# Sparse attention in a fused two-block kernel: the compression's value rows under the first scores, and the value products of a step in one group over eight buffers

## What is computed

```python
def compress(raw, j):                      # j = 0: keys, j = 1: values
    blk = raw[:, tok] + cmp_pos[j][None, None, :, None, :]
    blk = blk.transpose(0, 1, 3, 2, 4).reshape(B, n_cmp, N_KV_HEADS, CMP_BLOCK * HEAD_DIM)
    hid = jax.nn.gelu(blk @ cmp_w1[j] + cmp_b1[j])
    return hid @ cmp_w2[j] + cmp_b2[j]
...
s_cmp = jnp.einsum('btghd,bcgd->bghtc', q, k_cmp)
p_cmp = masked_softmax(s_cmp, cmp_end[None, :] <= pos[:, None])
o_cmp = jnp.einsum('bghtc,bcgd->btghd', p_cmp.astype(v_cmp.dtype), v_cmp)
...
o = gb[..., 0:1] * ocb + gb[..., 1:2] * o_sel + gb[..., 2:3] * o_win
```

## Time and profile before

| | before |
|---|---|
| median of 3 runs | 1528.6 us (1528.43 to 1529.43) |
| the profiled execution's own time | 1528.77 us |
| its span in the profile | 1527.1 us |
| TensorE busy | 1500.8 us, 98% |
| VectorE busy | 1067.8 us, 70% |
| ScalarE busy | 696.5 us, 46% |
| GpSimd busy | 271.9 us, 18% |
| granted TensorE clock | 0.999 |

### The profile page before, as it was taken

One profiled execution on the slowest core, in us unless ns is written; L12 is line 12 of the kernel. 1 busy time (PEld: TensorE's weight loads), 2 busy tenths in 40 slices (PEclk: granted clock), 3 DMA queues, 4 the chain that ended last, 5 costly groups with the idle time before them and its releaser, 6 DMA issues.

```text
span 1527.1 us, 20994 instructions
## 1 busy us (share of the span) xinstructions
PE 1500.8 (98%) x8228; PEld 1249.2 (82%) x8228; DVE 1067.8 (70%) x1617; ACT 696.5 (46%) x1206; POOL 271.9 (18%) x205
## 2 busy tenths in 40 slices
PE   6999999999999999989999999999999999999999
PEld 5788888888888897977878888888888898877777
DVE  6798689889988773259885685665635653688665
ACT  4453552322314454347775552332314443777761
POOL 0110013223232000059872011111100011010000
PEclk9999999999999999999999999999999999999999
DMA  9774257478585213330000254344432242111211
GB/s 340 269 263 164 83 212 261 168 250 300 187 285 183 91 53 131 118 116 2 2 2 29 83 193 164 111 153 160 144 108 86 91 162 83 56 55 63 86 74 56
DMA packets 114247, 207.54 MB, mean 136 GB/s; under 512 B 6361, under 2 KB 21990, under 8 KB 114150
## 3 DMA queue, kind: packets, MB, share of 16 engines
q1 hardware_dynamic: 113822, 206.09, 39.3%
q10 hardware_dynamic: 328, 0.12, 0.0%
HBM read 202.00 MB, written 4.19 MB: 135 GB/s over the span
## 4 chain that ended last, share of the span: by engine, by line
PE 95%; DVE 3%; ACT 1%; issue 1%; DMA 1%; SPq 0%; ACTq 0%; DVEq 0%
PE PS L2340 56%; PE PS L2293 20%; PE PS L2694 3%; PE PS L2721 2%; PE PS L2684 2%; PE PS L2501 1%; PE PS L2787 1%; PE PS L2624 1%; PE PS L2364 1%; PE PS L2772 1%; PE PS L2853 1%; PE PS L2875 1%; PE PS L2574 1%; DVE MROW L1448 1%; PE PS L2686 1%
## 5 line engine op out<-in xcount | busy, mean ns | idle before, releaser
L764 ACT ACTIVATE WH<-RAW 128x2048 fp32r<-128x2048 f32 (+1 forms) x102 | 191.2, 1885 | 338.8 <-DMA RAW<-in_ff_w_in_dram 221.2
L1327 DVE TENSOR_TENSOR WL<-RAW,WH 128x2048 fp32r<-128x2048 f32 (+1 forms) x98 | 249.1, 2565 | 73.2 <-ACT WH L764 72.9
L544 POOL PARTITION_ALL_REDUCE MROW<-MACC x25 | 118.5, 4739 | 591.0 <-DVE MACC L1362 504.4
L2340 PE MATMUL PS<-WH,HIDh 128*128 128x512 f32 (+1 forms) x576 | 217.7, 378 | 0.0
L2340 PE MATMUL PS<-WH,HIDl 128*128 128x512 f32 (+1 forms) x576 | 217.5, 378 | 0.0
L2340 PE MATMUL PS<-WL,HIDh 128*128 128x512 f32 (+1 forms) x576 | 217.5, 378 | 0.0
L2340 PE MATMUL PS<-HTh,WH 128*128 128x512 f32 (+1 forms) x520 | 202.6, 390 | 0.0
L2340 PE MATMUL PS<-HTl,WH 128*128 128x512 f32 (+1 forms) x520 | 202.6, 390 | 0.0
L2340 PE MATMUL PS<-HTh,WL 128*128 128x512 f32 (+1 forms) x520 | 202.5, 389 | 0.0
L2340 PEld LDWEIGHTS PS<-WH,HIDh 128*128 128x128 f32 x576 | 108.4, 188 | 20.5 <-issue 0.2
L2340 PEld LDWEIGHTS PS<-WL,HIDh 128*128 128x128 f32 x576 | 108.4, 188 | 20.2
(11 more groups left out here) (380 smaller groups left out, 3065.6 us busy)
## 6 DMA issues: line engine op xcount, KB each, us to landing
MRAW<-in_ada_w_dram SPq DMA_DIRECT2D x40, 1024.0 KB, 7.3
RAW<-in_ff_w_in_dram SPq DMA_DIRECT2D x32, 1024.0 KB, 5.3
RAW<-in_ff_w_out_dram SPq DMA_DIRECT2D x32, 1024.0 KB, 5.1
RAW<-in_w_in_dram SPq DMA_DIRECT2D x16, 1024.0 KB, 5.2
MRAW<-in_w_ada_dram SPq DMA_DIRECT2D x12, 1024.0 KB, 8.7
PIECE<-in_ada_w_dram SPq DMA_DIRECT2D x16, 512.0 KB, 9.8
MRAW<-in_kv_ada_w_dram SPq DMA_DIRECT2D x8, 1024.0 KB, 6.1
RAW<-in_kv_w_dram SPq DMA_DIRECT2D x6, 1024.0 KB, 5.6
```

Of the source, the lines that this page charges most:

```text
L544: pool.partition_all_reduce(MROW[:], acc[:], P, RADD).then_inc(m_red, 1)
L764: act.activation(rounded(u)[:, 0:width(u)], RAW[:, u % 4, 0:width(u)], ACT.Copy).then_inc(w_hi, 1)
L1327: dve.tensor_tensor(WL[:, u % 4, 0:width(u)], RAW[:, u % 4, 0:width(u)], rounded(u)[:, 0:width(u)].bitcast(F32), ALU.subtract).then_inc(w_ ...
L2340: mm = pe.matmul(po, a, b_, start=(k == 0 and i == 0), stop=(k == KT - 1 and i == len(ops) - 1), skip_group_check=len(ops) > 3)
```

## The change

It has three parts.

1. **The value rows move.** Half of `hidden_rows(1, 0)` goes behind the `W2K` products, and `hidden_rows(1, 1)` is cut into five pieces of 3, 3, 3, 3 and 4 products that go ahead of `scores(3)` to `scores(7)`. The gelu of the values is no longer taken from ScalarE's table: VectorE adds the biases and makes x + 0.044715 x^3 at t = 9 (`value_rows`), ScalarE takes exp of it at t = 10, VectorE finishes at t = 11 (`value_gelu`). The `W2V` products go from t = 3 to t = 14, VectorE's eviction of them from t = 5 to t = 15, GpSimd's copy of `VC` behind its weights of step 0, and the first product with `VC` to t = 18. The exp table is loaded right behind the second gelu of the keys.
2. **One group a step.** All products of L2721 of a step come at unit 6, in the order tile 1 branch 0, tile 1 branch 1, tile 0 branch 0, tile 0 branch 1. The turned weights have eight buffers in turn, two of them in the space of the queries of the first two pairs. A step raises the semaphore `a_pv` twice where it did three times.
3. **GpSimd** runs one small addition, whose result nobody reads, behind the reduction that ends at 486.5 us in the profile before. The buffers `PB` change places.

```diff
-    PB = [at(f"PB{i}", [P, 512], F32, o_rb + 2048 * i if i < 4 else o_mraw + 2048 * (i - 4)) for i in range(12)]
+    PB = [at(f"PB{i}", [P, 512], F32, o_mraw + 2048 * i if i < 8 else o_rb + 2048 * (i - 8)) for i in range(12)]
...
+    PT += [at(f"PT{6 + i}", [P, 512], F32, o_y + 2048 * i) for i in range(2)]
...
+        pool.tensor_tensor(SM[:, 47:48], EPST[:], EPST[:], ALU.add)
         pool.wait_ge(full, 4 * group_of["compress"])
...
+            if S == 0:
+                pool.wait_ge(kc_r, 3)
+                pool.tensor_copy(VC[32:64, :, HD:2 * HD], VC[0:32, :, 0:HD]).then_inc(vc_copies, 1)
+                pool.wait_ge(vc_copies, 1)
...
     def turned_of(u):
-        return PT[row(u) % 6] if u % PER else PTC[u // PER % 2]
+        return PT[row(u) % 8] if u % PER else PTC[u // PER % 2]
...
+        act.activation(SM[:, 44:45], EPST[:], ACT.Exp)
+        act.wait_ge(kc_f, 1)
...
+        def gelu_exp():
+
+            act.wait_ge(hc_b, 8)
+            act.activation(GE[:], GE[:], ACT.Exp, scale=-GELU_RATE * GELU_CUBE).then_inc(hc_b, 1)
...
+            if t == 10:
+                gelu_exp()
...
+        def value_rows():
+
+            dve.wait_ge(hc_f, 4)
+            dve.wait_ge(kc_f, 1)
+            b, v = SM[:, 42:44], HC[:].rearrange("p m (g c) -> p m g c", c=CMP)
+            ps = PS[:, 6:8, 1:129].rearrange("p m (g c) -> p m g c", c=32)[:, :, :, 0:CMP]
+            dve.tensor_tensor(b, PS[:, 6:8, 0], C1[:, C_B1 + 2:C_B1 + 4], ALU.add).then_inc(hc_b, 1)
+            dve.wait_ge(hc_b, 5)
+            dve.tensor_tensor(b, PS[:, 6:8, 128], b, ALU.add).then_inc(hc_b, 1)
+            dve.wait_ge(hc_b, 6)
+            for mo in range(2):
+                last = dve.tensor_scalar(v[:, mo], ps[:, mo], SM[:, 42 + mo:43 + mo], None, ALU.add)
+            last.then_inc(hc_r, 1)
+            dve.wait_ge(hc_r, 3)
+            dve.tensor_tensor(GE[:], HC[:], HC[:], ALU.mult).then_inc(hc_b, 1)
+            dve.wait_ge(hc_b, 7)
+            dve.scalar_tensor_tensor(out=GE[:], in0=GE[:], scalar=1.0 / GELU_CUBE, in1=HC[:],
+                                     op0=ALU.add, op1=ALU.mult).then_inc(hc_b, 1)
+
+        def value_gelu():
+
+            dve.wait_ge(hc_b, 9)
+            dve.tensor_scalar(GE[:], GE[:], 1.0, None, ALU.add).then_inc(hc_b, 1)
+            dve.wait_ge(hc_b, 10)
+            dve.reciprocal(GE[:], GE[:]).then_inc(hc_b, 1)
+            dve.wait_ge(hc_b, 11)
+            dve.tensor_tensor(HC[:], HC[:], GE[:], ALU.mult).then_inc(hc_r, 1)
...
-        hidden_rows(1, 0)
+        hidden_rows(1, 0, last=8)
...
-        hidden_rows(1, 1)
+        hidden_rows(1, 0, first=8)
...
-                pairs = ((1, 0, (u - 2, u)),) if i == 3 else ((1, 1, (u - 2, u)), (0, 0, (u - 4, u - 1)),
-                                                              (0, 1, (u - 4, u - 1)))
-                for blk, br, of in pairs:
+                for blk, br, of in ((1, 0, (u - 5, u - 3)), (1, 1, (u - 2, u)), (0, 0, (u - 4, u - 1)),
+                                    (0, 1, (u - 4, u - 1))):
...
+            if 3 <= t < 8:
+                hidden_rows(1, 1, 3 * (t - 3), 16 if t == 7 else 3 * (t - 2))
             if t < UNITS:
                 scores(t)
-            if t == 3:
+            if t == 14:
                 compressed_values()
-            if t == TURN_LAG:
+            if t == VALUES_LAG + 2:
                 pe.wait_ge(vc_copies, 1)
-            if 0 <= t - VALUES_LAG < UNITS and (t - VALUES_LAG) % PER in (0, 3, 6):
+                values(0)
+            elif t > VALUES_LAG and t - VALUES_LAG < UNITS and (t - VALUES_LAG) % PER in (0, 6):
                 values(t - VALUES_LAG)
```

More of the change, by code:

```diff
@@ L737, in summed @@
     def summed(u):
-        return 3 * (u // PER) + (1, 2, 3, 2, 3, 3, 3)[u % PER]
+        return 2 * (u // PER) + (2 if u % PER else 1)
     def before_in_pt(u):
-        return u - PER if u % PER else u - 2 * PER
+        if u % PER == 0:
+            return u - 2 * PER
+        r = row(u) - 8
+        return PER * (r // 6) + r % 6 + 1 if r >= 0 else -1
     SB_BANK, SB_COL, SB_AT = (0, 1, 0, 2), (0, 0, P, 0), (0, 512, P, 768)
@@ L1832, in dve_program, with hidden_bias @@
         chunk(kv_br(1), split=False)
-        def hidden_bias(j, mo):
-            ps, i = hidden(j, mo), 2 * j + mo
-            dve.wait_ge(hc_f, i + 1)
-            b = SM[:, 40 + i:41 + i]
-            dve.tensor_tensor(b, ps[:, 0:1], C1[:, C_B1 + i:C_B1 + i + 1], ALU.add).then_inc(hc_b, 1)
-            dve.wait_ge(hc_b, 2 * i + 1)
-            dve.tensor_tensor(b, ps[:, 128:129], b, ALU.add).then_inc(hc_b, 1)
-        hidden_bias(0, 0)
-        hidden_bias(0, 1)
-        hidden_bias(1, 0)
+        def hidden_bias(mo):
+            ps = hidden(0, mo)
+            dve.wait_ge(hc_f, mo + 1)
+            b = SM[:, 40 + mo:41 + mo]
+            dve.tensor_tensor(b, ps[:, 0:1], C1[:, C_B1 + mo:C_B1 + mo + 1], ALU.add).then_inc(hc_b, 1)
+            dve.wait_ge(hc_b, 2 * mo + 1)
+            dve.tensor_tensor(b, ps[:, 128:129], b, ALU.add).then_inc(hc_b, 1)
+        def value_rows():
[7 more added lines that the diff above has]
+            dve.wait_ge(hc_b, 6)
+            for mo in range(2):
+                last = dve.tensor_scalar(v[:, mo], ps[:, mo], SM[:, 42 + mo:43 + mo], None, ALU.add)
[12 more added lines that the diff above has]
+            dve.tensor_tensor(HC[:], HC[:], GE[:], ALU.mult).then_inc(hc_r, 1)
+        hidden_bias(0)
+        hidden_bias(1)
         dve.wait_ge(kc_full32, 1)
@@ L1850, in dve_program @@
         dve.tensor_tensor(KCl[:], KCF[:], KCh[:].bitcast(F32), ALU.subtract).then_inc(kc_r, 1)
-        hidden_bias(1, 1)
         def compressed_values():
@@ L1944, in dve_program @@
                 negmax(t)
-            if t == 5:
+            if t == 11:
+                value_gelu()
+            elif t == 15:
                 compressed_values()
@@ L2617, in pe_program, with hidden_rows @@
         chunk("A", HIDh, HIDl, mixed=True)
-        def hidden_rows(j, mo):
+        def hidden_rows(j, mo, first=0, last=16):
             pe.wait_ge((cw0_in, cw1_in[mo])[j], 16)
-            for m in range(16):
+            for m in range(first, last):
                 half = m // 8
@@ L2626, in hidden_rows @@
                                skip_group_check=True)
-            mm.then_inc(hc_f, 1)
+            if last == 16:
+                mm.then_inc(hc_f, 1)
         evicted(35)
```

39 lines of the change are left out of this document (18 added, 21 removed).

## The result

| | before | changed |
|---|---|---|
| median | 1528.84 us (1528.43 to 1529.43, 4 runs) | 1544.06 us (1543.17 to 1544.55, 4 runs) |
| the profiled execution's own time | 1528.77 us | 1544.13 us |
| its span | 1527.1 us | 1542.3 us |
| TensorE, VectorE, ScalarE, GpSimd busy | 1500.8, 1067.8, 696.5, 271.9 us | 1504.5, 1063.5, 696.2, 274.7 us |
| granted TensorE clock | 0.999 | 0.995 |

The ratio is 1.0098, 95% interval 1.0086 to 1.0111: slower by 15.2 us. The forecast was 1529.2 with an upper end of 1533.0, so it was wrong, and the cause has to be a large one.

The account below looks back on a forecast made before the run. TensorE's order, holes included, was taken to bound the kernel (95% of the chain of waits), with VectorE setting the pace at the loop's start. The terms -1.7 + 4.8 - 3.5 + 0.8 = +0.4 gave 1529.2 us, range 1525.3 to 1533.0.

Parts of the forecast that it names:

- part 2, one group a step: Attention steps: one group less costs TensorE 0.25 us less a step, over 14 steps 3.5 us earlier.
- Eight buffers are enough for no new wait: Attention steps: the copy of unit 3 needs only the group of the step before, written two iterations ahead; no cost.
- Rival 2: TensorE behind the long group: VectorE starves, steps stretch 0.3 us in each of 14, +4.2, 1533.4 us; chance 0.12.
- my own criterion: Attention steps: a step stretches once VectorE's 8.0 us of work and its idle exceed the new 8.8 us.
- Part 1 up to the first scores: Compression to first scores: 16 records instead of 32 lie before the scores, so they start 1.7 us earlier, at 665.64.
- Part 1, the start of the loop: Loop start to the group of t = 22: VectorE, full there, gets new work; 4.8 us later.
- The new work: VectorE at t = 9 and 11: additions, products and a reciprocal of 1.6 us for the value gelu, sum 4.2 us.
- The company on the port: Loop start: GpSimd's weights of step 0 beside four new VectorE operations cost 0.2 us each, 0.7 in all.
- rival 3: Loop start: each of four VectorE operations waits for a whole GpSimd operation, +2.5 and perhaps 1 more, 1532.7 us; chance 0.08.
- The tail: Last two attention steps: later group products cost 1.5 us, turns no longer waiting give back 0.7; 0.8 us later.
- Rival 1: Loop start: the value rows hide in VectorE's holes and TensorE limits t = 8 to 22; -3.5, 1525.3 us; chance 0.18.
- rival 4: GpSimd's early code load does not last, so staging ends at 666.8 as before; scores +1.3, 1530.6 us; chance 0.05.

Follow-up runs that it names:

- group_only: The kernel before with one group of value products a step and eight buffers, compression and gelus untouched; 1539.00 us.
- group_light: As `group_only`, with VectorE's scaling of units 3 and 6 left out; 1537.72 us.
- warm_only: The kernel before with GpSimd's one small addition alone; 1528.35 us.
- rows_only: The changed kernel with the two groups a step of the kernel before, over the eight buffers; 1533.62 us.
- rows_filled2: As `rows_only`, with unread TensorE products: ten ahead of the keys' products, four and six ahead of the scores of t = 12 and 13; 1531.20 us.
- before_copy13: The kernel before with the copies of turned weights one iteration earlier on ScalarE and VectorE; 1529.19 us.
- after_act13: The changed kernel with ScalarE's copies of turned weights alone one iteration earlier; 1535.15 us.

## Why the prediction was wrong, point by point

- **The step that failed: part 2, one group a step, -3.5 us.** Alone it measured +10.2 (`group_only`). The saving is real in TensorE's parts (4.66 us of groups in a pair against some 4.97, so 0.31 a pair where I had 0.5), but "Eight buffers are enough for no new wait" looked only at `PT`, where it was true. The wait came through the PSUM banks of the turned weights: `turn(u)` needs the copy of unit u - 3, and that copy stands on ScalarE behind an exp that the long group makes late. I had named both facts, the bank rule and the order of copies, and never put them in one chain.
- **Rival 2 had the mechanism half right, with a chance of 0.12 and a size of 0.3 a step.** The idle time behind the group was forecast at 1.4, from the 0.75 in a step whose next maximum has 256 columns; there it measured 1.50, and 1.24 in the other steps. By my own criterion, 8.0 of work and its idle against 8.8, the step had to stretch by 0.6; I weighed it down because an idle time elsewhere would go, and it did not (0.53 ahead of unit 0's maximum). The criterion itself was the wrong one, as `group_light` shows; it came near the size because both follow the same hole. Measured against the 8.8, the step stretched by 0.94.
- **Part 1 up to the first scores, -1.7.** The keys' products at 662.98 with a hole of 2.26 (forecast 663.3 and 2.6), the staging without a gap, the splits done in time: right, though the start of the keys' products differs by more than that from kernel to kernel (661.97 to 663.62 in the 20 traces), so that its closeness is partly luck. The first scores came at 666.22, not 665.64, and counted from the keys' products 3.24 behind them where I had 2.31, since those 16 records ran at the low clock. I saw a hole grow threefold and asked only what stands behind it.
- **Part 1, the start of the loop.** The new work, 4.2, measured 4.19, the reciprocal 1.70 against 1.6. The company on the port, 0.7, measured nothing on these rows: with GpSimd's weights from 677.02 to 683.09 beside them (`TENSOR_SCALAR`), the sum came out as forecast without it. So rival 3 fell here, and with it, for these operations, the strict reading of the Trainium skill (SBUF — State Buffer, Terms, "shared port pair": the loser is blocked for the other's whole instruction). Beside GpSimd's staging (`TENSOR_TENSOR` of 64x512, 1.3 us each) the trace agrees with it: the splits in `warm_only` and the 1.38 us in `group_light` above. Step 0's coefficients began at 676.20, not 675.5. The group's start, forecast 2.8 later, was 4.4 later in `rows_only` and 1.3 later in `rows_filled2`, where the clock held. Counted from the keys' products, which started at another time in each (663.33 before, 662.10, 662.32), it was 5.6 and 2.3 later. So with the clock up the forecast of this part was right to 0.5, and the missing term is the clock. TensorE's wait of 1.14 stood in the trace before too; the one of 1.48 is new, and I had not worked it out although VectorE's 4.2 us had to put it there. Behind the two came some six us at the low clock, and TensorE became the one that VectorE waited for.
- **The two parts together at the mark of t = 22** (the group's end) were 6.05 late, against 4.36 and 0.64 alone. The 1.05 on top are no work of the two on each other: counted from the keys' products it is 6.4, against 5.6 and 1.0.
- **The tail, +0.8** (0.2 to 1.5): +1.71 measured, and +1.72 in `group_only`. It is the long group's; with early copies 0.6 of it is left. `rows_only` has none.
- **Rival 1** needed VectorE's new rows to vanish in holes; **rival 4** needed the code to be loaded again. Neither happened.
- **The chances** were drawn too tight: the upper end of the range, 1533.0, fell 11 us short. The forecast stood on the claim that TensorE's order in the steps, once written, runs without waits, rival 2 gave up that claim for 0.3 a step, and no term had the clock in it.

## What to carry to other kernels

Before merging work on the engine that bounds into a longer block, follow the loop that feeds it (here scores, maximum, exp, copy, transposes) through every engine's order, and ask which instruction with old input stands behind one whose input the block makes late; a constant of that order can be worth more than the merge. A sum of an engine's work and idle time that equals the step proves nothing; take work away and see. When a change opens or widens holes on TensorE, price the stretch behind them at both levels of the clock.

## What was not expected of the hardware

- The granted clock stood at 0.51 from 664.0 to 667.2 us, behind a hole of 2.26 us that ended at 662.98, and near 0.50 for some six us behind waits of 1.14 and 1.48 us that came 1.1 us apart. Products without a reader in the holes went with 1.00 both times.
- The same waits do not always bring the fall. In the trace before, with a wait of 1.14 us that ends at 679.23, the clock stays at 1.00. In that of `before_copy13`, with one of 1.13 us that ends at 678.38, it falls for some three us, and so it does in five of the kernels with the long group; and behind the hole of 1.78 us in `after_act13` it stayed at 1.00. Of the 102 executions of the kernel before, ten have a mean clock of 0.998 or less, and they took 1530.03 to 1532.25 us.

```profile
679.00:681.00 2.00, 2.00 (x12) 1.65 (x11) 1.67 (x3) 1.54 (x8) 1.91 (x3) 0.51 0.00 0
```

- The hole named "issue" ahead of the keys' products ended between 661.97 and 663.62 in 19 traces, whatever stood ahead of it, which fits a DMA's landing; it was not tried apart. A mark behind it can be compared between two traces only when counted from it.
- The gap that goes with GpSimd's code load was 7.93 to 9.41 us in the 20 traces, and an idle stretch 160 us earlier hid it whole.
- VectorE beside GpSimd is slowed by some of its work and not by other: a 128x128 operation took 1.38 us instead of 0.29 beside the subtractions of the staging, and the new operations took 4.19 us in sum, as forecast without company, beside its scaling of weights.
- The reciprocal of 248 columns took 1.70 us, four times a product of as many.
